# A trunk layer step with split weights: low parts written over the raw tile, six buffers of high parts, splits five tiles ahead, experts in pairs

## The chip, the cores and the metric

The kernel runs on one core of one Trainium2 chip. The metric is the device time in microseconds of one execution. Engines are named as in the profile: PE is TensorE (PEld its weight loads), DVE is VectorE, ACT is ScalarE, POOL is GpSimd, SP is SyncE, which here issues nearly all DMAs.

## The reference, cut to what matters

Two layers over 272 prompt rows (16 meta tokens and 256) and 32 rows of running sequences, model width 1024, feed-forward width 2816, all in fp32:

```python
for i in range(2):
    h = pool_mixer(x) if i == 0 else conv_module(x)            # layer 1: two dense products and a 31-tap conv
    x = layer_norm(ALPHA * x + h)
    f = swiglu(x) if i == 0 else moe_swiglu(x)                 # top 2 of 8 experts
    x = layer_norm(ALPHA * x + f)

def swiglu(x, wg, wu, wd):
    return (silu(x @ wg) * (x @ wu)) @ wd

def moe_swiglu(x, router, wg, wu, wd):
    gate = softmax over the two largest of x @ router, 0 elsewhere
    return sum(gate[:, e] * swiglu(x, wg[e], wu[e], wd[e]) for e in range(8))
```

## The kernel before, in words

A product in fp32 is made of three products in a faster format (fp32r): each operand is split into a high part (a cast) and a low part (the operand minus the high part), and high by high, high by low and low by high are summed in PSUM. For weights this goes tile by tile. A tile is 128 x 2048 floats, 1 MB. SP loads it into one of 11 raw buffers (`RAW`; the dense stages use 4 of them, `DENSE`), ACT casts it into `w_hi` (`hi`, line 546), DVE subtracts into `w_lo` (`lo`, line 1185), and PE uses both. There are three pairs of `w_hi` and `w_lo` (`SPLIT`). Tiles are numbered in the order of their use, and four semaphores count them: `raw_landed`, `hi_ready`, `split_ready`, `tile_used`. A cast of tile t waits until tile t - 3 is used; a load into a raw buffer waits until the tile that was in it is split (`split_ready`).

The dense stages come first: 22 gate and up tiles, 11 down tiles, 8 tiles of the first and 4 of the second product of the conv module (T_DOWN, T_W1, T_W2 are their first numbers). A dense tile is 48 matmuls of 304 columns. For the conv module's 31 taps, ACT also builds diagonal matrices, some of them in buffers of `w_hi` and `w_lo` (`diag`).

Then come 8 experts of 33 tiles each (`TE`), from T_MOE on. Each expert's rows are gathered by a product with a selection matrix (`gather_rows`, `gather_turn`), so that an expert works on 128 rows. For each of 11 column blocks j there are a gate tile and an up tile (24 matmuls of 256 columns each: the wide tiles), a transposition of h (`turn_h`), and the down tile of the block before (12 matmuls of 512 columns). The result yy of an expert is split into yy_hi (ACT, line 795) and yy_lo (DVE, line 1583), spread back to all rows behind the next expert's first up tile (`scatter`, line 1073), and added into `acc` by DVE bank by bank (`add_scattered`, line 1533). The gate tile of block 1 writes the bank that the scatter filled first, so PE waits there for the first add.

Every engine has its own instruction stream in a written order; nothing is reordered by a scheduler. ACT and DVE run casts and subtractions two or three tiles ahead of PE (`AHEAD`), interleaved by hand with evacuations. Seven experts run in a hardware loop (`Fori`), one per turn, and the eighth is written out after it. A second pass for experts with more than 128 rows follows under an `If`, which is skipped here.

Of the kernel before, what the change touches and what calls it, by code (L numbers as in the profile page):

```python
# [33 lines left out]
RAW = 11  # L34
SPLIT = 3
LN_EPS = 1e-5
# [4 lines left out]
def build_trunk(nc, x_prompt, x_sample, state_pool, state_conv, meta, pool_w, pool_scale, conv_w1,  # L41
# [34 lines left out]
    TE = 3 * NJ  # L76
    assert TE % RAW == 0 and TE % SPLIT == 0

# [18 lines left out]
    with ExitStack() as ctx:  # L97

        ring_at = 16512
        split_at = ring_at + RAW * 8192  # L100
        const_at = split_at + 2 * SPLIT * 8192
        place = [const_at]
# [255 lines left out]
        A_U = A_CONV + len(U_JOBS)  # L358
        AHEAD = 3
        SCAT = 6 * (E + 1)  # L360
# [13 lines left out]
        def diag(j):  # L374
            if j < EARLY:
                return diag_h[j], diag_l[j]
            if j < EARLY + SPLIT:
                k = (T_W2 + j - EARLY) % SPLIT
                return w_hi[k], w_lo[k]
            return diag_h[j - EARLY - SPLIT], diag_l[j - EARLY - SPLIT]  # L380

# [3 lines left out]
        def _(sp):  # L385
            def load(t, src, dst):

                if t >= DENSE:
                    sp.wait_ge(split_ready, load_ahead(t) + 1)
                sp.dma_start(dst(raw[raw_slot(t)]), src).then_inc(raw_landed[raw_slot(t)], 16)  # L390
# [51 lines left out]

            def load_expert(n, e, j):
                t = T_MOE + j
                sp.wait_ge(split_ready, n * TE + (t - RAW + 1))
                src, dst = expert_tile(e, j) if j < TE else expert_tile(e + 1, j - TE)
                sp.dma_start(dst(raw[raw_slot(t)]), src).then_inc(raw_landed[raw_slot(t)], 16)
# [20 lines left out]
            def one_pass(r):  # L468
                with sp.Fori(0, E - 1) as e:
                    for j in range(LENT, TE + LENT):  # L470
                        load_expert(r * E + e, e, j)
                for j in range(LENT, TE):
                    load_expert(r * E + (E - 1), E - 1, j)

# [57 lines left out]
        def _(act):  # L532
# [3 lines left out]
            def hi(t, n=None):  # L536

                landed = 16 * (loads_before(t) + 1)
                if n is None:
                    act.wait_ge(raw_landed[raw_slot(t)], landed)  # L540
                    if t >= SPLIT:
                        act.wait_ge(tile_used, t - SPLIT + 1)
# [142 lines left out]
            for i in range(NW1 // 2):  # L685
                if i < NW1 // 2 - 1:
                    hi(T_W1 + 2 * i + 2)
                    hi(T_W1 + 2 * i + 3)
                else:
                    uc_split(0)  # L690
                    uc_split(1)
                    act.wait_ge(tile_used, T_W2 - SPLIT + 1)
# [11 lines left out]
            act.wait_ge(tile_used, T_W2 - SPLIT + 2)  # L704
            diagonals(EARLY + 1, 0, 32)
            for k, (part, half) in enumerate(U_JOBS):
# [3 lines left out]
                         ps[U_BANKS[k]][0:n, :]).then_inc(evac_a, 1)  # L710
            act.wait_ge(tile_used, T_W2 - SPLIT + 3)
            diagonals(EARLY + 2, 0, 32)
# [44 lines left out]

            def one_expert(r, e, last):

                n = r * E + e  # L760
                t0 = n * TE

                def silu(j, gate_tile):
# [33 lines left out]
            def one_pass(r):  # L797
                rows_evac(r * E)
                xg_evac(r * E)
                with act.Fori(0, E - 1) as e:  # L800
                    one_expert(r, e, False)
                one_expert(r, E - 1, True)

# [3 lines left out]
            with act.If(largest > P):  # L807
                with act.Fori(1, 3) as r:
                    for j in range(AHEAD):
                        hi(T_MOE + j, r * E)  # L810
# [9 lines left out]
        def _(pe):  # L820
# [83 lines left out]
            def feature_block(banks, n, t, blocks, x_base=None):  # L904

                wh, wl = wide(w_hi[t % SPLIT]), wide(w_lo[t % SPLIT])
                for c in range(KC):
# [27 lines left out]
            for i in range(NJ):  # L937
                t = T_DOWN + i
                pe.wait_ge(split_ready, t + 1)
                pe.wait_ge(jlo_done, i + 1)  # L940
                wh, wl = tall(w_hi[t % SPLIT]), tall(w_lo[t % SPLIT])
                for s in range(TR):
# [133 lines left out]

            def one_expert(r, e, last):

                n = r * E + e
                scattered = r * SCAT + e * 6  # L1080

                def rows_block(bank, j, t):

                    pe.wait_ge(split_ready, n * TE + (t + 1))
                    wh, wl = wide(w_hi[t % SPLIT]), wide(w_lo[t % SPLIT])
                    for c in range(KC):
# [13 lines left out]
                def down(j, t):  # L1100
                    pe.wait_ge(split_ready, n * TE + (t + 1))
                    pe.wait_ge(ht_lo_done, n * NJ + (j + 1))
                    wh, wl = tall(w_hi[t % SPLIT]), tall(w_lo[t % SPLIT])
                    for s in range(TR):
# [8 lines left out]
                for j in range(NJ):  # L1113
                    g = T_MOE + (3 * j - 1 if j else 0)
                    if j == 0:
# [34 lines left out]
                if not last:  # L1150
                    gather_turn(n + 1)
                down(NJ - 1, T_MOE + TE - 1)

            def one_pass(r):
                gather_rows(r * E)
                gather_turn(r * E)
                with pe.Fori(0, E - 1) as e:
                    one_expert(r, e, False)
                one_expert(r, E - 1, True)
                scatter((r * E + E) * 2 + r + 1)  # L1160
# [12 lines left out]
        def _(dve):  # L1173
# [369 lines left out]

            def one_expert(r, e, last):

                n = r * E + e

# [9 lines left out]

                lo(T_MOE + 3, n)
                mult(0, 1)
                dve.wait_ge(h_done, n * NJ + (FC + 1))  # L1560
                add_scattered(e, r * SCAT + e * 6, range(4))
                for j in range(1, NJ):
                    g = 3 * j - 1
                    lo(T_MOE + g + 2, n)
# [3 lines left out]
                    lo(T_MOE + g + 3, n)  # L1568
                    mult(j, g + 1)
                    if not last or j < NJ - 1:  # L1570
                        lo(T_MOE + g + 4, n)
                    if j == 2 and not last:
# [3 lines left out]
                if not last:  # L1576
                    xg_low(n + 1)
                    lo(T_MOE + TE + 1, n)
                    lo(T_MOE + TE + 2, n)
                for k in range(2):  # L1580
# [5 lines left out]
            def one_pass(r):  # L1586
                with dve.Fori(0, E - 1) as e:
                    one_expert(r, e, False)
                one_expert(r, E - 1, True)
                dve.wait_ge(summed, r * SCAT + 6 * E)  # L1590
# [16 lines left out]
            with dve.If(largest > P):  # L1607
                with dve.Fori(1, 3) as r:
# [6 lines left out]
                    select(0)  # L1615
                    for j in range(AHEAD):
                        lo(T_MOE + j, r * E)
# [47 lines left out]
```

## Time and profile before

| | us |
|---|---|
| median of 3 runs | 1303.0 (1302.25 to 1303.61) |
| the profiled execution | 1302.67 |
| its span | 1300.9 |
| PE busy | 1243.0 (96%) |
| DVE busy | 1027.0 (79%) |
| ACT busy | 825.3 (63%) |

The span is what the profiler sees between the first and the last instruction; the execution has 1.8 us around it. The dense stages take up to about 440 us, the experts run from 456 to 1277 us, and a last normalization ends at 1301. The busy share of an engine is a mean over these stages; what each engine waits for is read stage by stage.

### The profile page before, as it was taken

The numbers are of one execution on the slowest core, as the hardware profiler recorded it, in microseconds if no ns is written. First come the engines' busy times: TensorE is split into PE (matmuls) and PEld (weight loads), VectorE is DVE, ScalarE is ACT, GpSimd is POOL, SyncE is SP. The second block draws the span as 40 slices with busy tenths as digits, with TensorE's granted clock in tenths as the row PEclk, the third lists the DMA queues.
The fourth block names the chain that finished last, engine by engine and source line by source line (L and its number), as shares of the span: only waits on it lengthen the run. The fifth ranks groups of instructions, "written<-read, shape, count | busy, mean of one in ns | idle before, by whom it ended". The sixth has DMA issues, their size and how long they took to land.

```text
span 1300.9 us, 22335 instructions
## 1 busy us (share of the span) xinstructions
PE 1243.0 (96%) x8651; PEld 1158.3 (89%) x8651; DVE 1027.0 (79%) x1064; ACT 825.3 (63%) x979; POOL 5.4 (0%) x22
## 2 busy tenths in 40 slices
PE   6999999999998899999999999999999999999992
PEld 4899999989988689989989989989998999998991
DVE  6687444467996688888888888889889879888886
ACT  3636563344876657767767767767776776776771
POOL 0000000000000000000000000000000000000000
PEclk9999999999999999999999999999999999999997
DMA  9355544422565169989989989999999998998931
GB/s 252 98 167 177 154 153 155 147 85 65 174 216 182 65 212 366 362 280 366 365 276 361 364 292 352 364 316 322 365 322 318 367 353 284 367 362 278 367 117 38
DMA packets 249537, 332.65 MB, mean 256 GB/s; under 512 B 6404, under 2 KB 222820, under 8 KB 249450
## 3 DMA queue, kind: packets, MB, share of 16 engines
q1 hardware_dynamic: 249283, 331.28, 75.8%
q10 hardware_dynamic: 199, 0.62, 0.2%
q8 instruction: 36, 0.59, 0.2%
q14 instruction: 19, 0.16, 0.0%
HBM read 330.44 MB, written 2.84 MB: 256 GB/s over the span
## 4 chain that ended last, share of the span: by engine, by line
PE 84%; DVE 10%; ACT 3%; issue 2%; DMA 0%; DVEq 0%; SPq 0%; ACTq 0%
PE bank L1088 36%; PE bank L1108 19%; PE bank L915 17%; PE bank L946 6%; DVE cacc L1368 2%; PE bank L1052 2%; PE bank L1097 1%; PE bank L1073 1%; ACT w_hi L546 1%; PE bank L854 1%; DVE acc L1533 1%; PE bank L900 1%; DVE sg L1265 1%; DVE yy_lo L1583 1%; DVE w_lo L1185 1%
## 5 line engine op out<-in xcount | busy, mean ns | idle before, releaser
L1185 DVE TENSOR_TENSOR w_lo<-raw,w_hi 128x2048 fp32r<-128x2048 f32 x309 | 707.8, 2291 | 184.3 <-ACT w_hi L546 183.6
L546 ACT CAST w_hi<-raw 128x2048 fp32r<-128x2048 f32 x309 | 591.1, 1914 | 226.1 <-PE bank L915 76.5
L1088 PE MATMUL bank<-w_hi,xg_hi 128*128 128x256 f32 x1408 | 400.7, 285 | 5.5 <-DVE acc L1533 3.7
L1088 PE MATMUL bank<-w_hi,xg_lo 128*128 128x256 f32 x1408 | 393.3, 279 | 0.0
L1088 PE MATMUL bank<-w_lo,xg_hi 128*128 128x256 f32 x1408 | 393.1, 279 | 0.0
L1088 PEld LDWEIGHTS bank<-w_hi,xg_hi 128*128 128x128 f32 x1408 | 264.5, 188 | 13.3 <-issue 9.1
L1088 PEld LDWEIGHTS bank<-w_lo,xg_hi 128*128 128x128 f32 x1408 | 265.0, 188 | 3.2
L1088 PEld LDWEIGHTS bank<-w_hi,xg_lo 128*128 128x128 f32 x1408 | 264.2, 188 | 0.0
L915 PE MATMUL bank<-x_hi,w_hi 128*128 128x304 f32 (+1 forms) x544 | 166.0, 305 | 6.9 <-DVE x_lo L1272 3.6
L915 PE MATMUL bank<-x_hi,w_lo 128*128 128x304 f32 (+1 forms) x544 | 164.0, 302 | 0.0
L915 PE MATMUL bank<-x_lo,w_hi 128*128 128x304 f32 (+1 forms) x544 | 163.2, 300 | 0.0
L1108 PE MATMUL bank<-w_hi,ht_hi 128*128 128x512 f32 x352 | 139.1, 395 | 1.3 <-DVE ht_lo L1555 1.0
L1108 PE MATMUL bank<-w_lo,ht_hi 128*128 128x512 f32 x352 | 138.2, 393 | 0.0
L1108 PE MATMUL bank<-w_hi,ht_lo 128*128 128x512 f32 x352 | 137.8, 392 | 0.0
L770 ACT CAST ht_hi<-bank 128x256 fp32r<-128x256 f32 x88 | 32.8, 373 | 135.3 <-PE bank L1097 135.3
L915 PEld LDWEIGHTS bank<-x_hi,w_hi 128*128 128x128 f32 x544 | 102.2, 188 | 9.0 <-issue 6.3
L915 PEld LDWEIGHTS bank<-x_lo,w_hi 128*128 128x128 f32 x544 | 102.5, 188 | 0.1
L915 PEld LDWEIGHTS bank<-x_hi,w_lo 128*128 128x128 f32 x544 | 102.3, 188 | 0.0
L1108 PEld LDWEIGHTS bank<-w_hi,ht_lo 128*128 128x128 f32 x352 | 66.2, 188 | 14.8
L1108 PEld LDWEIGHTS bank<-w_hi,ht_hi 128*128 128x128 f32 x352 | 66.1, 188 | 14.6 <-DVE ht_lo L1555 2.0
L1108 PEld LDWEIGHTS bank<-w_lo,ht_hi 128*128 128x128 f32 x352 | 66.2, 188 | 11.0
L946 PE MATMUL bank<-h_hi,w_hi 128*128 128x304 f32 x176 | 55.0, 313 | 1.9 <-DVE h_lo L1342 1.9
(202 smaller groups left out, 1279.5 us busy)
## 6 DMA issues: line engine op xcount, KB each, us to landing
raw<-in_moe_w_gate_dram SPq DMA_DIRECT2D x88, 1024.0 KB, 5.6
raw<-in_moe_w_up_dram SPq DMA_DIRECT2D x88, 1024.0 KB, 6.0
raw<-in_moe_w_down_dram SPq DMA_DIRECT2D x88, 1024.0 KB, 5.2
raw<-in_conv_w_dram SPq DMA_DIRECT2D x12, 1024.0 KB, 5.6
raw<-in_ffn_w_gate_dram SPq DMA_DIRECT2D x11, 1024.0 KB, 5.3
raw<-in_ffn_w_up_dram SPq DMA_DIRECT2D x11, 1024.0 KB, 5.4
raw<-in_ffn_w_down_dram SPq DMA_DIRECT2D x11, 1024.0 KB, 4.9
poolw<-in_pool_w_dram SPq DMA_DIRECT2D x1, 1024.0 KB, 10.8
```

Source lines behind the costliest of these rows:

```text
L546: act.copy(w_hi[t % SPLIT][:], raw[raw_slot(t)][:]).then_inc(hi_ready, 1)
L770: act.copy(ht_hi[:], ps[4 + j % 2][:, 0:TR * P].rearrange("p (c n) -> p c n", c=TR))\
L854: last = pe.matmul(ps[0][:, 0:n], mean_mat[:], z(c), start=(c == first), stop=(c == end))
L900: last = pe.matmul(ps[1][:, 0:n], mean_mat[:], sq[:, c, 0:n], start=(c == 0), stop=(c == KC - 1))
L915: last = pe.matmul(bank[:, 0:n], w[:, c, cols], x[:, c, 0:n], start=(c == 0 and k == 0), stop=(c == KC - 1 and k == 2))
L946: last = pe.matmul(ps[c][:, 0:NT], w[:, s, cols], x[i % 2][:, s, :], start=(i == 0 and s == 0 and k == 0), stop=(i == NJ - 1 and s == TR - ...
L1052: last = pe.matmul(ps[1 + 2 * half][:, :], sel[:, i, :], x[:, i, half * HALF:(half + 1) * HALF], start=(i == 0 and m == 0), stop=(i == 2 a ...
L1073: last = pe.matmul(ps[SCATTER_BANKS[k]][0:n, :], sel_t[:, P * i:P * i + n], y[:, half * HALF:(half + 1) * HALF], start=(m == 0), stop=(m = ...
L1088: last = pe.matmul(bank[:, 0:TW], x[:, c, :], w[:, c, :], start=(c == 0 and k == 0), stop=(c == KC - 1 and k == 2))
L1108: last = pe.matmul(ps[6 + half][:, :], x[:, s, :], w[:, s, cols], start=(j == 0 and s == 0 and k == 0), stop=(j == NJ - 1 and s == TR - 1 ...
L1185: dve.tensor_tensor(w_lo[t % SPLIT][:], raw[raw_slot(t)][:], w_hi[t % SPLIT][:], ALU.subtract).then_inc(split_ready, 1)
L1368: ins = dve.scalar_tensor_tensor(out=out, in0=src, scalar=v(V_DW + KC * k + q), in1=out, op0=ALU.mult, op1=ALU.add)
```

## The change

`w_lo` now lies at the addresses of `raw`, so the subtraction overwrites the raw tile, and the room that it had makes six buffers of `w_hi` (`HIGH`). A cast of tile t waits until tile t - 6 is used. A load into a raw buffer waits until the tile that was in it is used, not split. In the experts ACT and DVE run five tiles ahead (`AHEAD = 5`; three are split before the experts, as before, and two more on entering them). A buffer's number depends on the tile's number modulo 6 and an expert has 33 tiles, so the loops' bodies now hold two experts (`side` 0 and 1): three turns, and the last two experts are written out. The diagonal matrices of the conv module use six `w_hi` buffers in place of three pairs.

```diff
-SPLIT = 3
+HIGH = 6
-        w_hi = [at(f"w_hi{i}", [P, 2048], F32R, split_at + 16384 * i) for i in range(SPLIT)]
-        w_lo = [at(f"w_lo{i}", [P, 2048], F32R, split_at + 16384 * i + 8192) for i in range(SPLIT)]
+        w_lo = [at(f"w_lo{i}", [P, 2048], F32R, ring_at + 8192 * i) for i in range(RAW)]
+        w_hi = [at(f"w_hi{i}", [P, 2048], F32R, split_at + 8192 * i) for i in range(HIGH)]
-        AHEAD = 3
+        AHEAD = 5
+        EARLY_TILES = 3
 # SP
-                    sp.wait_ge(split_ready, load_ahead(t) + 1)
+                    sp.wait_ge(tile_used, load_ahead(t) + 1)
-                sp.wait_ge(split_ready, n * TE + (t - RAW + 1))
+                sp.wait_ge(tile_used, n * TE + (t - RAW + 1))
-                with sp.Fori(0, E - 1) as e:
-                    for j in range(LENT, TE + LENT):
-                        load_expert(r * E + e, e, j)
+                with sp.Fori(0, E // 2 - 1) as d:
+                    for j in range(LENT, 2 * TE + LENT):
+                        load_expert(r * E + 2 * d, 2 * d, j)
 # ACT, the cast
-                    act.wait_ge(tile_used, n * TE + (t - SPLIT + 1))
-                act.copy(w_hi[t % SPLIT][:], raw[raw_slot(t)][:]).then_inc(hi_ready, 1)
+                    act.wait_ge(tile_used, n * TE + (t - HIGH + 1))
+                act.copy(w_hi[t % HIGH][:], raw[raw_slot(t)][:]).then_inc(hi_ready, 1)
 # ACT, one expert (DVE alike, with lo)
+                def ahead(j):
+                    if not last or j < TE:
+                        hi(m0 + j, pair)
-                hi(T_MOE + 3, n)
+                ahead(AHEAD)
                 silu(0, 0)
                 for j in range(1, NJ):
                     g = 3 * j - 1
-                    hi(T_MOE + g + 2, n)
+                    ahead(g + AHEAD - 1)
                     turn_evac(j - 1)
...
-                    hi(T_MOE + g + 3, n)
+                    ahead(g + AHEAD)
                     silu(j, g)
-                    if not last or j < NJ - 1:
-                        hi(T_MOE + g + 4, n)
+                    ahead(g + AHEAD + 1)
...
-                    hi(T_MOE + TE + 1, n)
-                    hi(T_MOE + TE + 2, n)
+                ahead(TE + AHEAD - 2)
+                ahead(TE + AHEAD - 1)
 # PE (ACT and DVE alike)
-                with pe.Fori(0, E - 1) as e:
-                    one_expert(r, e, False)
-                one_expert(r, E - 1, True)
+                with pe.Fori(0, E // 2 - 1) as d:
+                    for side in range(2):
+                        one_expert(r, 2 * d, side, False)
+                for side in range(2):
+                    one_expert(r, E - 2, side, side == 1)
 # DVE, the subtraction
-                dve.tensor_tensor(w_lo[t % SPLIT][:], raw[raw_slot(t)][:], w_hi[t % SPLIT][:],
+                dve.tensor_tensor(w_lo[raw_slot(t)][:], raw[raw_slot(t)][:], w_hi[t % HIGH][:],
                                   ALU.subtract).then_inc(split_ready, 1)
```

The order on DVE (VectorE) where one expert ends and the next begins, before: two subtractions, the two halves of yy_lo, the loop's jump, one subtraction, then the product hn of block 0. The digits behind a name are the buffer and its place in the program.

```order
L1185 TENSOR_TENSOR w_lo1_64<-raw5_54,w_hi1_61 128x2048 [waits hi_ready]
L1184 REGISTER_ALU
L1185 TENSOR_TENSOR w_lo2_65<-raw6_55,w_hi2_62 128x2048 [waits hi_ready]
L1581 ISA
L1583 TENSOR_TENSOR yy_lo_140<-bank6,yy_hi_139 128x512 [waits yy_hi_done]
L1581 REGISTER_ALU
L1583 TENSOR_TENSOR yy_lo_140<-bank7,yy_hi_139 128x512 [waits yy_hi_done]
L1587 REGISTER_ALU
L1587 COMPARE_AND_BRANCH
L1185 TENSOR_TENSOR w_lo0_63<-raw7_56,w_hi0_60 128x2048 [waits hi_ready]
```

The same place in the changed kernel, between the two experts of a pair:

```order
L1201 TENSOR_TENSOR w_lo7_67<-raw7_56,w_hi3_74 128x2048 [waits hi_ready]
L1200 REGISTER_ALU
L1201 TENSOR_TENSOR w_lo8_68<-raw8_57,w_hi4_75 128x2048 [waits hi_ready]
L1603 ISA
L1605 TENSOR_TENSOR yy_lo_151<-bank6,yy_hi_150 128x512 [waits yy_hi_done]
L1603 REGISTER_ALU
L1605 TENSOR_TENSOR yy_lo_151<-bank7,yy_hi_150 128x512 [waits yy_hi_done]
L1200 REGISTER_ALU
L1201 TENSOR_TENSOR w_lo9_69<-raw9_58,w_hi5_76 128x2048 [waits hi_ready]
```

The order is the same; the tiles are two later ones, `w_lo7` has the place of `raw7`, and there is no jump inside a pair.

The order on ACT (ScalarE) at the same boundary, before: two casts, the two halves of yy_hi, the jump, one cast, silu of block 0.

```order
L545 REGISTER_ALU [waits raw_landed5]
L546 CAST w_hi1_61<-raw5_54 128x2048 [waits tile_used]
L545 REGISTER_ALU [waits raw_landed6]
L546 CAST w_hi2_62<-raw6_55 128x2048 [waits tile_used]
L795 CAST yy_hi_139<-bank6 128x512 [waits tile_used]
L795 CAST yy_hi_139<-bank7 128x512
L800 REGISTER_ALU
L800 COMPARE_AND_BRANCH
L546 CAST w_hi0_60<-raw7_56 128x2048 [waits tile_used,raw_landed7]
```

And in the changed kernel, between the two experts of a pair:

```order
L548 REGISTER_ALU [waits raw_landed7]
L549 CAST w_hi3_74<-raw7_56 128x2048 [waits tile_used]
L548 REGISTER_ALU [waits raw_landed8]
L549 CAST w_hi4_75<-raw8_57 128x2048 [waits tile_used]
L801 REGISTER_ALU
L803 CAST yy_hi_150<-bank6 128x512 [waits tile_used]
L803 CAST yy_hi_150<-bank7 128x512
L549 CAST w_hi5_76<-raw9_58 128x2048 [waits tile_used,raw_landed9]
```

Here too the order stands; the buffers `w_hi3` to `w_hi5` are new, and each cast's wait for `tile_used` names an earlier tile than before.

## Rows read from the trace of the kernel before

**Rows 1.** The page, busy time of each engine (share of the span) and instructions.
```profile
PE 1243.0 (96%) x8651; PEld 1158.3 (89%) x8651; DVE 1027.0 (79%) x1064; ACT 825.3 (63%) x979; POOL 5.4 (0%) x22
```

**Rows 2.** Windows of the dense stage and one expert: us, busy, clock, DMA share, GB/s.
```profile
100.00:260.00 160.00, 158.07 (x1124) 157.85 (x1124) 77.79 (x54) 80.23 (x136) 0.00 (x0) 0.99 0.48 154
...
864.00:967.00 103.00, 102.40 (x718) 94.66 (x719) 89.33 (x68) 72.75 (x64) 0.00 (x0) 1.00 0.99 336
```

**Rows 3.** Waits from 864 to 967: who waited for whom, us, times, longest.
```profile
ACT ht_hi L770 <- PE bank L1097: 16.8, 11, 4.9
...
ACT w_hi L546 <- PE bank L1108: 8.2, 10, 0.8
...
PE bank L1088 <- DVE acc L1533: 0.5, 1, 0.5
```

**Rows 4.** Timeline of ACT between two experts: start, us, instruction [idle before].
```profile
864.52 1.92 ACT L546 CAST w_hi<-raw 128x2048 fp32r<-128x2048 f32 x1
867.07 1.91 ACT L546 CAST w_hi<-raw 128x2048 fp32r<-128x2048 f32 x1 [0.64 <-PE bank L1108]
868.89 1.07 ACT L795 CAST yy_hi<-bank 128x512 fp32r<-128x512 f32 x2
```

**Rows 5.** Timeline of DVE at the same place.
```profile
866.46 2.29 DVE L1185 TENSOR_TENSOR w_lo<-raw,w_hi 128x2048 fp32r<-128x2048 f32 x1 [1.00 <-ACT w_hi L546]
869.02 2.29 DVE L1185 TENSOR_TENSOR w_lo<-raw,w_hi 128x2048 fp32r<-128x2048 f32 x1 [0.26 <-ACT w_hi L546]
...
872.43 2.28 DVE L1185 TENSOR_TENSOR w_lo<-raw,w_hi 128x2048 fp32r<-128x2048 f32 x1
874.63 0.41 DVE L1551 TENSOR_TENSOR hn<-sgn,bank 128x256 f32<-128x256 f32 x1
875.27 1.41 DVE L1533 SCALAR_TENSOR_TENSOR acc<-bank,gate,acc 128x512 f32<-128x512 f32 x2 [0.23 <-PE bank L1073]
```

**Rows 6.** Timeline of PE behind the scatter of that boundary.
```profile
875.20 0.40 PE L1073 MATMUL bank<-yy_lo,sel_t 128*32 128x512 f32 x1
876.15 0.39 PE L1088 MATMUL bank<-w_hi,xg_hi 128*128 128x256 f32 x1 [0.55 <-DVE acc L1533]
```

**Rows 7.** Timeline of DVE in the first expert.
```profile
456.02 0.91 DVE L1602 MEMSET yy_hi<- 128x1024 f32 x1 [0.16 <-issue]
...
463.91 1.41 DVE L1533 SCALAR_TENSOR_TENSOR acc<-bank,gate,acc 128x512 f32<-128x512 f32 x2 [0.24 <-DVE hn L1551]
```

**Rows 8.** Timeline of DVE in a normalization: one in place, one not.
```profile
286.90 0.53 DVE L1279 SCALAR_TENSOR_TENSOR zT<-zT,vec,sg 128x304 f32<-128x304 f32 x1
287.35 0.53 DVE L1272 SCALAR_TENSOR_TENSOR x_lo<-zT,vec,x_hi 128x304 fp32r<-128x304 f32 x1
```

**Rows 9.** All loads into raw buffers, time from issue to landing.
```profile
DMA to landing us min/median/max: 4.7/5.6/15.6
```

**Rows 10.** Timeline of PE: first and last matmuls of experts' first tiles.
```profile
866.64 0.39 PE L1108 MATMUL bank<-w_hi,ht_lo 128*128 128x512 f32 x1
866.87 0.28 PE L1088 MATMUL bank<-w_hi,xg_hi 128*128 128x256 f32 x1
...
869.58 0.28 PE L1088 MATMUL bank<-w_hi,xg_lo 128*128 128x256 f32 x1
...
969.76 0.28 PE L1088 MATMUL bank<-w_hi,xg_hi 128*128 128x256 f32 x1
...
972.36 0.28 PE L1088 MATMUL bank<-w_hi,xg_lo 128*128 128x256 f32 x1
...
1072.64 0.28 PE L1088 MATMUL bank<-w_hi,xg_hi 128*128 128x256 f32 x1
...
1175.52 0.28 PE L1088 MATMUL bank<-w_hi,xg_hi 128*128 128x256 f32 x1
```

**Rows 11.** Timeline of DVE behind the skipped second pass.
```profile
1290.21 0.34 DVE L1624 BATCH_NORM_AGGREGATE mv<-stats 128x2 f32<-128x12 f32 x3 [3.78 <-issue]
```

**Rows 12.** The page, one instruction queue: packets, MB, share.
```profile
q8 instruction: 36, 0.59, 0.2%
```

More of the change, by code:

```diff
@@ L76, in build_trunk @@
     TE = 3 * NJ
-    assert TE % RAW == 0 and TE % SPLIT == 0
+    assert 2 * TE % RAW == 0 and 2 * TE % HIGH == 0
     DENSE = 4
@@ L756, in rows_evac, with one_expert @@
                     act.copy(xg_rows[:, k * HALF:(k + 1) * HALF], ps[1 + 2 * k][:, :]).then_inc(rows_out, 1)
-            def one_expert(r, e, last):
-                n = r * E + e
+            def one_expert(r, first, side, last):
+                pair = r * E + first
+                n = pair + side
                 t0 = n * TE
+                m0 = T_MOE + side * TE
+                def ahead(j):
+                    if not last or j < TE:
+                        hi(m0 + j, pair)
                 def silu(j, gate_tile):
@@ L799, in one_pass @@
                 xg_evac(r * E)
-                with act.Fori(0, E - 1) as e:
-                    one_expert(r, e, False)
-                one_expert(r, E - 1, True)
+                for j in range(EARLY_TILES, AHEAD):
+                    hi(T_MOE + j, r * E)
+                with act.Fori(0, E // 2 - 1) as d:
+                    for side in range(2):
+                        one_expert(r, 2 * d, side, False)
+                for side in range(2):
+                    one_expert(r, E - 2, side, side == 1)
             one_pass(0)
@@ L808, in _ @@
                 with act.Fori(1, 3) as r:
-                    for j in range(AHEAD):
+                    for j in range(EARLY_TILES):
                         hi(T_MOE + j, r * E)
@@ L1075, in scatter, with one_expert @@
                     last.then_inc(spread, 1)
-            def one_expert(r, e, last):
-                n = r * E + e
-                scattered = r * SCAT + e * 6
+            def one_expert(r, first, side, last):
+                pair = r * E + first
+                n = pair + side
+                m0 = T_MOE + side * TE
+                scattered = r * SCAT + (first + side) * 6
                 def rows_block(bank, j, t):
-                    pe.wait_ge(split_ready, n * TE + (t + 1))
-                    wh, wl = wide(w_hi[t % SPLIT]), wide(w_lo[t % SPLIT])
+                    pe.wait_ge(split_ready, pair * TE + (t + 1))
+                    wh, wl = wide(w_hi[t % HIGH]), wide(w_lo[raw_slot(t)])
                     for c in range(KC):
@@ L1100, in down @@
                 def down(j, t):
[L1101 removed]
+                    pe.wait_ge(split_ready, pair * TE + (t + 1))
                     pe.wait_ge(ht_lo_done, n * NJ + (j + 1))
[L1103 removed]
+                    wh, wl = tall(w_hi[t % HIGH]), tall(w_lo[raw_slot(t)])
                     for s in range(TR):
@@ L1151, in one_expert @@
                     gather_turn(n + 1)
-                down(NJ - 1, T_MOE + TE - 1)
+                down(NJ - 1, m0 + TE - 1)
             def one_pass(r):
@@ L1156, in one_pass @@
                 gather_turn(r * E)
-                with pe.Fori(0, E - 1) as e:
-                    one_expert(r, e, False)
-                one_expert(r, E - 1, True)
+                with pe.Fori(0, E // 2 - 1) as d:
+                    for side in range(2):
+                        one_expert(r, 2 * d, side, False)
+                for side in range(2):
+                    one_expert(r, E - 2, side, side == 1)
                 scatter((r * E + E) * 2 + r + 1)
@@ L1542, in xg_low, with one_expert, ahead @@
                                       xg_hi[:, 4 * k:4 * k + 4, :], ALU.subtract).then_inc(xg_lo_done, 1)
-            def one_expert(r, e, last):
-                n = r * E + e
+            def one_expert(r, first, side, last):
+                pair = r * E + first
+                n = pair + side
+                e = first + side
+                m0 = T_MOE + side * TE
+                def ahead(j):
+                    if not last or j < TE:
+                        lo(m0 + j, pair)
                 def mult(j, up_tile):
@@ L1563, in one_expert @@
                     g = 3 * j - 1
-                    lo(T_MOE + g + 2, n)
+                    ahead(g + AHEAD - 1)
                     if j == 1:
@@ L1567, in one_expert @@
                     turn_low(j - 1)
-                    lo(T_MOE + g + 3, n)
+                    ahead(g + AHEAD)
                     mult(j, g + 1)
-                    if not last or j < NJ - 1:
-                        lo(T_MOE + g + 4, n)
+                    ahead(g + AHEAD + 1)
                     if j == 2 and not last:
@@ L1586, in one_pass @@
             def one_pass(r):
-                with dve.Fori(0, E - 1) as e:
-                    one_expert(r, e, False)
-                one_expert(r, E - 1, True)
+                for j in range(EARLY_TILES, AHEAD):
+                    lo(T_MOE + j, r * E)
+                with dve.Fori(0, E // 2 - 1) as d:
+                    for side in range(2):
+                        one_expert(r, 2 * d, side, False)
+                for side in range(2):
+                    one_expert(r, E - 2, side, side == 1)
                 dve.wait_ge(summed, r * SCAT + 6 * E)
@@ L1615, in _ @@
                     select(0)
-                    for j in range(AHEAD):
+                    for j in range(EARLY_TILES):
                         lo(T_MOE + j, r * E)
```

38 lines of the change are left out of this document (19 added, 19 removed).

## The prediction

> **What bounds the kernel now.** I read the page's head first, then the windows by stage, then the waits of one expert, then the three engines' timelines around the change from one expert to the next.
>
> The head says that TensorE is busy 96% of the span [rows 1]. The windows say where the other 4% are not: a stretch of 103 us in the expert loop, about one expert, has 102.3 us of matmuls, and 160 us of the dense stage have 158.1 [rows 2]. So both long stages run at TensorE's pace, and whatever makes a split or a load earlier can only give back the gaps. The waits of one expert show how small these are [rows 3]: ScalarE's casts wait 8.2 us behind TensorE's down tiles alone for a buffer of high parts, but that is an engine ahead of schedule. TensorE itself is in the list with 0.5 us behind a VectorE add, and nowhere behind `split_ready`. The change removes waits of ScalarE and VectorE which TensorE does not feel, except where a chain through those two engines ends at TensorE. That is at the start of each expert.
>
> **The boundary of two experts, step by step.** ScalarE casts two tiles ahead (864.52 and 867.07), then the two halves of yy_hi [rows 4]. VectorE subtracts for the same two tiles, makes yy_lo, subtracts one more tile, multiplies hn, and then adds bank 1 into acc [rows 5]. TensorE needs bank 1 for the second gate tile, and starts it at 876.15 after 0.55 us of marked idle, released by this add [rows 6]; from its last scatter matmul, one matmul pace (0.23) after 875.20, the gap is 0.7 us.
>
> In this chain one wait goes. The second cast sat 0.64 us until TensorE had used the last down tile, since with three buffers tile t needs tile t-3 used. With six it needs t-6, used two tiles earlier, so the cast starts right behind the first. VectorE gains less than 0.64: its first subtraction (866.46) still waits for the first cast, which waits for nothing that changes. Two subtractions in a row start 2.20 us apart (872.43 to 874.63), so the second can start at 868.66 and not 869.02: 0.36 us; the bracket in its row says 0.26. I take 0.35. All behind it on VectorE follows directly: yy_hi, right behind the cast, is made 0.6 earlier than 868.89, and so is the cast for the next subtraction, so neither stops VectorE. The add is 0.35 earlier, and TensorE's tile starts at 875.80. What is late next is the add still, behind the third subtraction: the scatter ends near 875.4, so 0.4 us of the gap stays. Seven boundaries: 7 x 0.35 = **2.45 us gained** (1.8 to 2.5).
>
> **The first expert loses.** Before, VectorE had one subtraction between clearing yy_hi (456.02) and the first add at 463.91 [rows 7]. Now it has three there, since tiles 3 and 4 are split on entry and tile 5 in the expert. The clearing ends at 456.93; no cast waits for TensorE any more; three subtractions at 2.20 end their turn at 463.55, and the add comes 0.64 later, as 874.63 to 875.27 [rows 5]: 464.2. That is **0.3 us lost** (0 to 0.5).
>
> **Edits that I cost at nothing.** Writing the low part over its raw values: a subtraction in place should take what it took. The nearest rows are two scalar_tensor_tensor of one size, one in place (zT over zT) and one not (x_lo), 0.53 us both [rows 8]. Bounds: 0, and 0.1 us on each of the four subtractions in the boundary chain, +3 us in all.
>
> A raw slot now comes free when TensorE has used the tile and not when VectorE has split it. In the expert loop a load thus starts about a tile and a half later, and its cast is wanted 11 - 6 = 5 tiles after that, some 15 us at a mean of 103/33 = 3.1 us a tile. A load lands 5.6 us after its issue in the median and 15.6 at worst, which was at the start of the program [rows 9]. A late one eats lead of the splits first, and there are five tiles of that. In the dense stage a load now waits until the tile four before it is used; a tile there is 48 matmuls of 160/1124 = 0.142 us, 6.8 us [rows 2], so three tiles are 20 us against 5.6 + 1.9 + 2.3 of load, cast and subtraction. SP stands behind the waiting load with nothing but later loads, which need the same event later. If that cover were gone, each late tile would stop TensorE for the excess; I see no stretch where it is.
>
> The orders of ScalarE and VectorE inside an expert shift by two tiles, but the evacuations keep their places: ScalarE comes to ht_hi with time to spare (16.8 us of waiting for TensorE per expert [rows 3]), and VectorE spends 89.4 us of 103 [rows 2]; ht_lo stays as late behind its split as before.
>
> **The paired loop.** A pair's body runs as long as two experts, so there are two jumps back in place of six. The jumps cost nothing that I can see: expert starts follow each other by 102.89, 102.88 and 102.88 us, and the last of these was left without a jump [rows 10]. So nothing is gained by removing four. A jump over a body twice as long has no row. From below it is 0. From above it is the one place where an engine sits with only a long skip and a register load before it, 3.78 us of "issue" on VectorE before L1624 [rows 11]. If TensorE's jump is read while its last down tile of 12 matmuls runs, that covers 12 x 0.23 = 2.76 us (the step from 866.64 to 866.87 [rows 10]), and the 0.4 to 0.6 us of gap before the second gate tile swallows some more. So at the upper row a jump costs 3.78 - 2.76 - 0.6 = 0.4 us, two jumps **0.8 us**, which I take; 0 to 7.6 is kept for the range.
>
> Here the Trainium skill speaks against the change (Runtime: NRT & Kernel Launch, section Instruction fetch mechanics): TensorE's instruction memory holds 2048 instructions, refilled in blocks of 256, and a taken branch to a target outside what is held stalls until it has been fetched. One expert is about 720 matmuls with a weight load each, 1440, and fits; a pair is 2880 and does not. The trace agrees for the kernel before: its one large instruction queue moved 36 packets, 0.59 MB, which at the page's 16 KiB a block is some 9,200 instructions, while TensorE ran 2 x 8651 [rows 1, 12], so the loop was not fetched again on each turn. The page gives no price for the stall; by the rule there are two of them.
>
> **Sum.** -2.45 + 0.3 + 0.8 = -1.35 us on the profiled execution's 1302.67 (span 1300.9 and 1.8 around it): 1301.3. The median of the three runs is 1303.0, 0.3 above; on that, **1301.6 us**. What this measurement can tell from no change is about 0.2%, 2.6 us: the forecast is no change that can be told, on the fast side.
>
> **Rivals.**
> 1. *TensorE's pace moves.* The wide tiles of 24 matmuls come in two paces at the same granted clock of 1.00 [rows 2]: 2.71 us from first to last matmul (866.87 to 869.58) or 2.60 (969.76 to 972.36) [rows 10]. I count 138 of 176 at the slower one. No view says what sets it; the same tile of the loop has either. The faster ones lie mostly in the first third of an expert, after a stop, which may mean that how casts, subtractions and loads fall against the matmuls plays a part, and the change moves all three. If the 134 slow tiles not hidden behind the boundary chain all turned fast: 134 x 0.11 = 14.7 us, with the boundary 1287; a third of them, 1297. Against it: the first tile of an expert is split well ahead in each of them, and has either pace. The other way, some 26 fast tiles turned slow cost 2.9 us, 1304.5.
> 2. *The jump over the pair stalls in full, and the time is slower.* If TensorE's queue does not run past the jump, or VectorE's and ScalarE's own longer bodies stall too, two jumps cost up to 3.78 each, 7.6 in all: 1303.0 - 2.15 + 7.6 = 1308.4. It decides from an uncovered 1.1 us per jump on. For it: the skip's 3.78 is a real row, and VectorE's chain at the boundary has no slack, so a stall there goes straight through. Against it: the jumps of before cost nothing, on any of the engines.
> 3. *The change does nothing at the boundary*, because the first cast, the yy chain or the scatter is what counts after all: 1303 to 1304, with the first expert's loss and jumps.
> 4. *Subtractions in the ring or late loads stop TensorE*: +3 to +6 us, 1304 to 1307.
>
> **How the numbers follow.** Forecast, 1299.5 to 1303.5: 0.50, of which a fifth is more than 2.6 us faster. Pace faster, 1288 to 1299.5: 0.22. Jump stall, 1302.5 to 1309: 0.17, most of it over 1305.6. Rival 3: 0.04. Rival 4 and a slower pace, 1303.5 to 1307: 0.07. So faster 0.33, same 0.47, slower 0.20. The range 1294 to 1308 leaves out the deep end of the faster pace (about 0.1) and the worst stall (under 0.1).
>
> **What would show it.** In the profile after: ScalarE's waits for TensorE before casts nearly gone in the expert loop, with TensorE's busy time per expert as before; the second cast at a boundary directly behind the first; the tile after the scatter 0.35 us nearer to it; experts 102.5 us apart; expert starts at odd and even places of the pair showing what a jump costs. The forecast is wrong if wide tiles change their pace in number, if TensorE waits for `split_ready`, or if every second boundary is longer by microseconds.

## The result and the profile after

| | before | after |
|---|---|---|
| median | 1303.6 us (7 runs, 1302.25 to 1307.45) | 1311.1 us (7 runs, 1308.10 to 1313.72) |
| the profiled execution, its span | 1302.67, 1300.9 | 1312.02, 1310.3 |

The ratio over all runs is 1.0048 with a 95% interval of 1.003 to 1.0065, which is some 6 us; between the medians it is 7.5. The changed kernel is slower, where 1301.6 and a chance of 0.20 for slower were forecast. Its median lies above the forecast's range (1294 to 1308) and above the 1308.4 of rival 2. Of the later runs, one of before (2501.7 us) and one of e7 (3174.6 us) fell into a slow state and are in no figure below.

The page of after, the lines that answer to [rows 1, 12], and the subtraction's group (busy, mean ns):

```profile
PE 1248.0 (95%) x8651; PEld 1164.1 (89%) x8651; DVE 1017.1 (78%) x1064; ACT 807.7 (62%) x979; POOL 5.4 (0%) x22
...
q8 instruction: 76, 1.25, 0.4%
...
L1201 DVE TENSOR_TENSOR w_lo<-raw,w_hi 128x2048 fp32r<-128x2048 f32 x309 | 700.3, 2287 | 174.1 <-ACT w_hi L549 173.7
```

The instruction queue moved 76 packets and not 36. The subtraction in place takes 2287 ns, as it took before (2291 in the same line of before's page). The busy time of TensorE grew by 5 us with the same number of instructions, so some ran slower; 4.4 us of the span are idle on top.

Most of the idle time lies where the loop turns; the busy time grew there and in the first expert. The waits of after from 864 to 967, the stretch of [rows 3], list something that before does not have: TensorE idle with nothing that releases it.

```profile
PEld bank L1102 <- issue: 3.8, 1, 3.8
DVE hn L1574 <- PE bank L1102: 3.4, 1, 3.4
PE bank L1102 <- issue: 3.4, 1, 3.4
```

TensorE's timeline of after at that place, the boundary of [rows 10] between the fourth and the fifth expert, where the loop jumps back (start, us, instruction, idle before):

```profile
873.23 0.40 PE L1122 MATMUL bank<-w_hi,ht_lo 128*128 128x512 f32 x1
877.01 0.46 PE L1102 MATMUL bank<-w_hi,xg_hi 128*128 128x256 f32 x1 [3.38 <-issue]
877.27 0.42 PE L1102 MATMUL bank<-w_lo,xg_hi 128*128 128x256 f32 x1
877.49 0.41 PE L1102 MATMUL bank<-w_hi,xg_lo 128*128 128x256 f32 x1
877.70 0.41 PE L1102 MATMUL bank<-w_hi,xg_hi 128*128 128x256 f32 x1
...
881.33 0.28 PE L1102 MATMUL bank<-w_hi,xg_lo 128*128 128x256 f32 x1
881.44 0.28 PE L1102 MATMUL bank<-w_hi,xg_hi 128*128 128x256 f32 x1
...
886.92 0.28 PE L1102 MATMUL bank<-w_hi,xg_hi 128*128 128x256 f32 x1
```

The down tile's last matmul and the next tile's first were 0.23 us apart; now it is 3.78. The tile behind the stall takes 4.43 us (877.01 to 881.44) instead of 2.83. In what follows, the boundary is the time from the last down matmul of one expert to the first matmul of the next one's second gate tile: 13.69 us here (873.23 to 886.92), before 9.51 (866.64 to 876.15 [rows 10, 6]). Windows of after say why (the stretch and its length, busy time and instructions of PE, PEld, DVE, ACT and POOL, granted clock, DMA share, GB/s): the dense stage, the stall, the tile behind it, the tile after that, and the start of the first expert.

```profile
100.00:260.00 160.00, 158.07 (x1124) 157.85 (x1123) 76.58 (x54) 81.03 (x134) 0.00 (x0) 0.99 0.47 152
...
873.90:877.00 3.10, 0.00 (x0) 0.00 (x0) 3.10 (x2) 2.18 (x4) 0.00 (x0) 1.00 0.68 229
877.00:881.40 4.40, 4.38 (x24) 4.39 (x25) 3.94 (x4) 1.60 (x1) 0.00 (x0) 0.61 0.27 108
881.40:884.20 2.80, 2.80 (x27) 2.80 (x27) 0.00 (x0) 2.18 (x2) 0.00 (x0) 1.00 0.36 81
...
450.00:461.00 11.00, 8.10 (x35) 6.50 (x34) 6.32 (x16) 7.41 (x9) 0.00 (x0) 0.69 0.00 1
```

TensorE stands still for 3.4 us, and then the granted clock is 0.61: most of the tile runs at the lower level, 1.2 GHz, where a matmul of 256 columns takes 0.21 us and not 0.11. Then it is back at 1.00. The last row shows a low clock where there is no jump, in the gather and the first tile of the first expert; before had 1.00 in it:

```profile
450.00:461.00 11.00, 8.10 (x61) 7.16 (x60) 4.06 (x15) 4.78 (x8) 0.00 (x0) 1.00 0.00 1
```

At a boundary inside a pair there is no stall, and what was forecast is there. After, ScalarE and VectorE between the third and the fourth expert, and TensorE behind the scatter, to be held against [rows 4, 5, 6]:

```profile
768.68 3.73 ACT L549 CAST w_hi<-raw 128x2048 fp32r<-128x2048 f32 x2
772.30 1.08 ACT L803 CAST yy_hi<-bank 128x512 fp32r<-128x512 f32 x2
```
```profile
770.63 4.49 DVE L1201 TENSOR_TENSOR w_lo<-raw,w_hi 128x2048 fp32r<-128x2048 f32 x2 [1.00 <-ACT w_hi L549]
...
776.25 2.28 DVE L1201 TENSOR_TENSOR w_lo<-raw,w_hi 128x2048 fp32r<-128x2048 f32 x1
778.45 0.41 DVE L1574 TENSOR_TENSOR hn<-sgn,bank 128x256 f32<-128x256 f32 x1
779.08 2.73 DVE L1549 SCALAR_TENSOR_TENSOR acc<-bank,gate,acc 128x512 f32<-128x512 f32 x4 [0.22 <-DVE hn L1574]
```
```profile
770.81 0.39 PE L1122 MATMUL bank<-w_hi,ht_lo 128*128 128x512 f32 x1
...
779.22 0.40 PE L1085 MATMUL bank<-yy_lo,sel_t 128*32 128x512 f32 x1
779.96 0.38 PE L1102 MATMUL bank<-w_hi,xg_hi 128*128 128x256 f32 x1 [0.34 <-DVE acc L1549]
```

The two casts are one block, the two subtractions too, and TensorE's idle time before the second gate tile went from 0.55 to 0.34. The boundary takes 9.15 us (770.81 to 779.96), before 9.50 or 9.51 at all boundaries in the loop and 9.24 at the one behind it: 0.36 less, where 0.35 was forecast. Its last part, from the first scatter matmul on, is 3.27 us (776.69 to 779.96), before 3.58 or 3.59; but that part is also longer when the two tiles ahead of it run at the faster of their paces and the scatter starts earlier, so the whole boundary is the better measure.

**Where 9.4 us of span went**, by comparing the starts of the tiles in the two profiles. The first expert, up to its second gate tile: +2.6, since its low clock costs 3.0 up to the scatter and TensorE, being late, then saves 0.4 of waiting. The two jumps: 3.50 of stall, 1.37 of slow tile, 0.22 more in the up tile behind it and 0.81 of waiting for the add that the stall swallows make +4.28 at the first, 3.55 + 1.59 - 0.14 - 0.82 = +4.18 at the second, 8.5 together. The five boundaries without a jump: -0.38, -0.36, -0.37, -0.62 and -0.41, which is -2.1; the fourth of these lies in the loop before and behind it after. What is left of the whole span is +0.4, of which 0.3 arose before the experts.

### The profile page after: what moved, and what is told of

Read it like the earlier page. It is cut to its first block, busy times and chain, and to the rows that moved or that the text cites. A ratio compares the mean times of both kernels' runs of the same rounds, so it can differ in the third digit from the quotient of the medians.

```text
span 1310.3 us, 22137 instructions
## 1 busy us (share of the span) xinstructions
PE 1248.0 (95%) x8651; PEld 1164.1 (89%) x8651; DVE 1017.1 (78%) x1064; ACT 807.7 (62%) x979; POOL 5.4 (0%) x22
## 4 chain that ended last, share of the span: by engine, by line
PE 85%; DVE 10%; ACT 3%; issue 2%; DMA 0%; DVEq 0%; ACTq 0%; SPq 0%
PE bank L1102 38%; PE bank L1122 18%; PE bank L927 17%; PE bank L958 6%; DVE cacc L1384 2%; PE bank L1064 2%; PE bank L1111 1%; DVE w_lo L1201 1%; PE bank L1085 1%; ACT w_hi L549 1%; PE bank L866 1%; PE bank L912 1%; DVE sg L1281 1%; DVE acc L1549 1%; DMA xin<-in_x_prompt_dram 0%
## 5 line engine op out<-in xcount | busy, mean ns | idle before, releaser
L1201 DVE TENSOR_TENSOR w_lo<-raw,w_hi 128x2048 fp32r<-128x2048 f32 x309 | 700.3, 2287 | 174.1 <-ACT w_hi L549 173.7
L549 ACT CAST w_hi<-raw 128x2048 fp32r<-128x2048 f32 x309 | 582.3, 1916 | 106.5 <-DMA raw<-in_ffn_w_up_dram 40.1
L927 PEld LDWEIGHTS bank<-x_lo,w_hi 128*128 128x128 f32 x544 | 102.4, 188 | 0.1
```

The costliest lines, as they stand in the source:

```text
L549: act.copy(w_hi[t % HIGH][:], raw[raw_slot(t)][:]).then_inc(hi_ready, 1)
L927: last = pe.matmul(bank[:, 0:n], w[:, c, cols], x[:, c, 0:n], start=(c == 0 and k == 0), stop=(c == KC - 1 and k == 2))
L1201: dve.tensor_tensor(w_lo[raw_slot(t)][:], raw[raw_slot(t)][:], w_hi[t % HIGH][:], ALU.subtract).then_inc(split_ready, 1)
```

## The experiments

Theory A: TensorE's program for a pair of experts no longer stays where one expert's did, so it is fetched again after each jump back, and TensorE waits for it; the deeper splits bring what was forecast. Theory B: the low parts in the ring, and raw slots that come free later, cost the time. Others are named with the run that tests them. In each table row below, "before" is the kernel before in the same set of runs: 1305.0 us in the first four (31 runs), 1305.4 in the last four (34 runs). e1 has 8 runs, e7 11, the others 12.

| | median us | ratio to before, 95% interval |
|---|---|---|
| e1, before with a loop over pairs | 1309.3 | 1.0034, 1.002 to 1.0049 |
| e2, after written out on all engines | 1302.3 | 0.9976, 0.9965 to 0.9987 |
| e3, six buffers and five ahead in a loop over one expert | 1305.5 | 1.0002, 0.9992 to 1.0011 |
| e4, before with low parts in place | 1304.8 | 0.9999, 0.9988 to 1.0011 |
| e5, after, TensorE alone written out | 1301.5 | 0.9972, 0.9955 to 0.9989 |
| e6, after, all but TensorE written out | 1309.7 | 1.0037, 1.0023 to 1.0051 |
| e7, before written out | 1303.3 | 0.9987, 0.9969 to 1.0004 |
| e8, as e3 but four ahead | 1302.6 | 0.9979, 0.9967 to 0.9992 |

**e1: the loop over pairs alone.** On each engine of the kernel before (cut; SyncE likewise with its loads):

```diff
-with pe.Fori(0, E - 1) as e:
-    one_expert(r, e, False)
+with pe.Fori(0, E // 2 - 1) as d:
+    for side in range(2):
+        one_expert(r, 2 * d + side, False)
+one_expert(r, E - 2, False)
 one_expert(r, E - 1, True)
```

> The kernel before with one edit: the loop's body holds two experts (two jumps back instead of six on each engine); three high and three low buffers, splits three tiles ahead, raw slots freed by the split. Theory A (the two jumps back over the pair stall TensorE, about 3.5 us idle and 1.5 us of half clock each, less 0.8 of the boundary's gap): 1303.6 + 2 x 4.2 = 1312 us, q8 instruction about 76 packets, and TensorE idle at the boundaries before the third and the fifth expert and at no other. Theory B (the low parts in the raw slots, and the slots freed later, cost the time): 1303.6. Theory C (the first expert's lower clock is brought by the deeper splits): the first expert at full clock here, whatever the total.

Measured: 1309.3, 4.3 us above before, and 76 packets in the queue. The place is right, the price was too high. The second jump in e1's timeline of TensorE, and the windows of this stall and of the tile behind it:

```profile
872.34 0.40 PE L1113 MATMUL bank<-w_hi,ht_lo 128*128 128x512 f32 x1
875.25 0.38 PE L1093 MATMUL bank<-w_hi,xg_hi 128*128 128x256 f32 x1 [2.52 <-DVE w_lo L1192]
...
884.05 0.38 PE L1093 MATMUL bank<-w_hi,xg_hi 128*128 128x256 f32 x1
```
```profile
872.30:875.20 2.90, 0.44 (x2) 0.00 (x1) 2.65 (x2) 2.42 (x3) 0.00 (x0) 1.00 0.24 81
875.20:878.10 2.90, 2.85 (x24) 2.85 (x25) 2.90 (x3) 0.45 (x1) 0.00 (x0) 1.00 0.84 243
```

The stall is 2.5 us here and not 3.4 (the releaser in its bracket is inferred; the tile that TensorE starts was split long before). The clock stays at 1.00. This boundary takes 11.71 us (872.34 to 884.05) and the one of the first jump 11.81, against 9.51: 2.3 and 2.2 us for the jumps, 4.5 in all, and a boundary that now lies behind the loop gives 0.26 back. That is 4.2, and the medians are 4.3 apart. So the loop alone makes the kernel slower, without any other part of the change. Theory B's 1303.6 is out. Theory C falls too: e1 has no deeper splits, and the first expert's low clock is in its profile (0.71 from 450 to 461).

**e2: no loop.** In all four engines of after, in the first pass (in outline, SyncE likewise with its loads):

```diff
-with pe.Fori(0, E // 2 - 1) as d:
-    for side in range(2):
-        one_expert(r, 2 * d, side, False)
+for d in range(E // 2 - 1):
+    for side in range(2):
+        one_expert(r, 2 * d, side, False)
```

> The kernel after without its loop: the eight experts of the first pass are written out on all four engines, buffers and lookahead as after. Theory A: no jump back, so no stall at the boundaries, 1311.1 - 8.4 = 1302.7 us if the first expert's half clock (2.9 us) stays, 1300 if it was chance; 0.35 us gained at each of the seven boundaries. Theory B (the in-place low parts cost the time): 1311. Theory D (code that is read for the first time stalls TensorE as a jump does): 1311 or more, with idle time before every expert.

Measured: 1302.3, with 71 packets, nearly as many as after. TensorE's first boundary in e2:

```profile
556.89 0.39 PE L1136 MATMUL bank<-w_hi,ht_lo 128*128 128x512 f32 x1
557.11 0.28 PE L1116 MATMUL bank<-w_hi,xg_hi 128*128 128x256 f32 x1
...
565.71 0.38 PE L1116 MATMUL bank<-w_hi,xg_hi 128*128 128x256 f32 x1
```

No stall stands at any boundary, so the packets alone cost nothing that can be seen where the code runs straight on; only the jump waits. Theory D falls. All boundaries take 8.82 us, 0.69 less than in the loop before, which is nearly twice the forecast 0.35; e7 says where the rest is from.

**e3: the loop over one expert with six buffers.** 33 tiles do not divide by six, so the order of the buffers is a table (cut; a cast waits for the tile that last had its buffer, and the other engines loop alike):

```diff
+HIGH_OF = [j % 6 if j < 18 else (j - 18) % 5 for j in range(TE)]
-act.copy(w_hi[t % HIGH][:], raw[raw_slot(t)][:])
+act.copy(w_hi[high(t)][:], raw[raw_slot(t)][:])
-with act.Fori(0, E // 2 - 1) as d:
+with act.Fori(0, E - 1) as e:
```

> The kernel after with a loop over one expert as in the kernel before: the six high buffers are taken in the order 0 to 5 three times, then 0 to 4 three times, so that 33 tiles close the cycle and a buffer comes back after at least five tiles. In-place low parts and splits five tiles ahead stay. Theory A: the body fits again, so q8 instruction is near 36 packets, no stall, 1303.6 - 7 x 0.35 = 1301 us (1304 if the first expert's half clock is brought by the deeper splits). Theory B: 1309 to 1311.

Measured: 1305.5, the same as before, 36 packets, no stall, and no gain: the boundaries take 9.51 us as before. The miss has its reason in ScalarE's timeline of e3 at the first boundary:

```profile
558.94 1.92 ACT L558 CAST w_hi<-raw 128x2048 fp32r<-128x2048 f32 x1
561.50 1.92 ACT L558 CAST w_hi<-raw 128x2048 fp32r<-128x2048 f32 x1 [0.64 <-PE bank L1129]
```

At the end of an expert the table gives a buffer back after five tiles, and five ahead of the last down tile means waiting for that tile: the wait of [rows 4] to the hundredth. Depth alone is worth nothing here; what counts, as e8 shows, is that no cast at the boundary waits for the last down tile. (Its profile has the first expert's low clock as well, 0.69.)

**e4: low parts in place alone.** In the kernel before (cut; the dense stages' loads wait for `tile_used` too, and the diagonal matrices get buffers in the room of `w_lo`):

```diff
-w_lo = [at(f"w_lo{i}", [P, 2048], F32R, split_at + 16384 * i + 8192) for i in range(SPLIT)]
+w_lo = [at(f"w_lo{i}", [P, 2048], F32R, ring_at + 8192 * i) for i in range(RAW)]
-sp.wait_ge(split_ready, n * TE + (t - RAW + 1))
+sp.wait_ge(tile_used, n * TE + (t - RAW + 1))
```

> The kernel before with one edit: the low part is written over the raw values and a load waits until TensorE has used the tile; three high buffers, splits three tiles ahead, a loop over one expert stay. Theory A: 1303.6, the same within 0.2%; subtraction 2.29 us as before. Theory B (in-place writing or the later freeing costs the time): 1309 to 1311.

Measured: 1304.8 against 1305.0, the same. This is theory B's own test, and it falls.

**e5 and e6: whose jump.** The edit of e2 on TensorE alone (e5), and on the other three engines alone (e6).

> The kernel after, with the first pass written out for TensorE alone; ScalarE, VectorE and SyncE keep the loop over pairs. Theory A (it is TensorE's own jump that stalls): no idle 3.4 us before the third and the fifth expert, 1311.1 - 2 x 4.2 = 1302.7 us. Theory E (the jump of another engine holds TensorE up at the same place): at least one of the two stalls stays, 1306 to 1311.

> The kernel after, with the first pass written out for ScalarE, VectorE and SyncE; TensorE alone keeps the loop over pairs. Theory A: both stalls stay, 1302.3 (all written out) + 2 x 4.2 = 1310.7 us. Theory E: they go, 1302 to 1306.

Measured: 1301.5 and 1309.7, theory A's numbers to within 1.2 us. TensorE's timelines at the boundary of the second and the third expert in e5, and of the fourth and the fifth in e6:

```profile
659.95 0.39 PE L1122 MATMUL bank<-w_hi,ht_lo 128*128 128x512 f32 x1
660.18 0.28 PE L1102 MATMUL bank<-w_hi,xg_hi 128*128 128x256 f32 x1
```
```profile
870.39 0.39 PE L1136 MATMUL bank<-w_hi,ht_lo 128*128 128x512 f32 x1
874.11 0.50 PE L1116 MATMUL bank<-w_hi,xg_hi 128*128 128x256 f32 x1 [3.33 <-issue]
```

With TensorE written out nothing stands at the boundary, though the three others jump there; with TensorE alone in a loop the stall is whole. The windows of e6 show the tile behind each of its two stalls at a low clock again:

```profile
664.80:669.10 4.30, 4.29 (x24) 4.29 (x25) 3.97 (x4) 0.62 (x1) 0.00 (x0) 0.64 0.22 88
...
874.10:878.60 4.50, 4.49 (x25) 4.49 (x26) 4.00 (x4) 0.65 (x1) 0.00 (x0) 0.62 0.23 93
```

**e7: before, written out.** The edit of e2 in the kernel before.

> The kernel before with the first pass written out on all four engines; its three high and three low buffers and splits three tiles ahead stay. Theory F (part of what the written-out kernel gained at a boundary comes from the loop itself: the boundary that before has behind its loop took 3.22 us against 3.58 in it): six boundaries at 3.22, 1305.0 - 6 x 0.36 = 1302.8 us. Theory G (all of it comes from the deeper splits): 1305.0.

Measured: 1303.3, a ratio whose interval just reaches 1, with all boundaries at 9.29 or 9.30 us in its profile:

```profile
559.57 0.39 PE L1119 MATMUL bank<-w_hi,ht_lo 128*128 128x512 f32 x1
...
565.64 0.47 PE L1084 MATMUL bank<-yy_hi,sel_t 128*128 128x512 f32 x1 [0.24 <-DVE yy_lo L1598]
...
568.86 0.38 PE L1099 MATMUL bank<-w_hi,xg_hi 128*128 128x256 f32 x1 [0.21 <-DVE acc L1548]
```

So theory F holds in kind: writing out is worth 0.21 us a boundary by itself (9.51 to 9.30). From the first scatter matmul on it is the 3.22 us expected, 0.36 less than before, but the scatter itself starts later, after a wait for yy_lo, and 0.15 of the gain goes there. Six boundaries make 1.3 us and not 2.2; the total, 2.0 less than before, is not told from no change. The freed cast is worth 0.36 in the loop (after) and 0.48 written out (9.30 here to e2's 8.82), so each helps the other a little, and together they are e2's 0.69. In the loop the semaphore values are worked out in registers, written out they are constants; whether that is the 0.21, or something else about the loop, was not tried.

**e8: four ahead.** One number of e3:

```diff
-        AHEAD = 5
+        AHEAD = 4
```

> The one-expert loop with six high buffers, in place, but splits four tiles ahead instead of five: with buffers that come back after five tiles the last cast at a boundary then waits for the tile before the last down tile, not for that tile itself (in the run with five ahead this cast waited 0.64 us for the last down tile as in the kernel before, and the boundary took 3.58 us as before). Theory A: boundaries 3.58 to 3.27 in the loop and 3.22 to 2.95 behind it, 1305.0 - 6 x 0.31 - 0.27 = 1302.9 us. Theory H (the loop over one expert, not the cast's wait, keeps the boundary at 3.58): 1305.

Measured: 1302.6, a ratio of 0.9979, theory A. ScalarE's timeline at the first boundary, and TensorE's at the first and the sixth:

```profile
558.25 1.91 ACT L558 CAST w_hi<-raw 128x2048 fp32r<-128x2048 f32 x1
560.05 1.07 ACT L812 CAST yy_hi<-bank 128x512 fp32r<-128x512 f32 x2
```
```profile
558.57 0.39 PE L1129 MATMUL bank<-w_hi,ht_lo 128*128 128x512 f32 x1
...
566.99 0.40 PE L1092 MATMUL bank<-yy_lo,sel_t 128*32 128x512 f32 x1
567.72 0.38 PE L1109 MATMUL bank<-w_hi,xg_hi 128*128 128x256 f32 x1 [0.34 <-DVE acc L1554]
...
1070.88 0.39 PE L1129 MATMUL bank<-w_hi,ht_lo 128*128 128x512 f32 x1
...
1080.03 0.38 PE L1109 MATMUL bank<-w_hi,xg_hi 128*128 128x256 f32 x1 [0.54 <-DVE acc L1554]
```

No cast waits before yy_hi, TensorE's idle time at the first boundary is 0.34 as in the changed kernel, and that boundary takes 9.15 us (558.57 to 567.72). So do all six in the loop (9.15 or 9.16), and the one behind it takes 8.89: 0.35 less than before at each of the seven, which is the forecast's 2.45 us. At the sixth the idle time is 0.54, as before, since its first two tiles ran 0.2 us faster and TensorE came to the wait earlier; the boundary is the same (1070.88 to 1080.03). Theory H falls. This is the change's idea in a loop that fits, 2.8 us faster than before between the medians (1.0 to 4.3 by the interval). e2 and e5 are faster than both kernels too; e5 has the lowest median, and the three were not compared with each other closely enough to rank them.

## Why the prediction was wrong

**The step that failed** is the jump. The prediction said: "If TensorE's jump is read while its last down tile of 12 matmuls runs, that covers 12 x 0.23 = 2.76 us", and took 0.4 us a jump. There is no such cover: the idle time begins when the down tile ends (873.23 to 877.01 in after), and it is 3.4 us, bare, not far below the upper row's 3.78 [rows 11]. On top came what no term had: the tile behind the stall at a lower clock, 1.4 and 1.6 us. A jump cost 4.28 and 4.18 us, where the sum had 0.4 for each; two of them are 7.7 us more than the sum had. e5 shows that this is TensorE's jump and no other's, and e1 that it needs no other part of the change.

The reason against rival 2, "the jumps of before cost nothing", was read from jumps whose target was still held: 36 packets with six jumps back, 76 with two, and in before the queue moves no packet from 560 to 1180 us, over five jumps back. By the Trainium skill (Runtime: NRT & Kernel Launch, section Instruction fetch mechanics) a taken branch whose target is not in the current two-page window stalls until the target's page has been fetched; the traces of after, e1 and e6 agree, at 2.5 to 3.4 us a time. In before, e3 and e8 the body, one expert with about 718 matmuls and as many weight loads [rows 2], is longer than two of that section's blocks of 256 instructions, and the jump is free: there the traces differ, and for TensorE more than two blocks are held. The prediction had this rule, counted that a pair does not fit, and then priced it by a cover that it had not seen.

**The boundary's gain** was right in kind and size where it could show. The second cast stands right behind the first, yy_lo and the add come earlier, and the boundaries inside a pair in the loop are 0.36 to 0.38 shorter against 0.35 forecast; e8 shows the gain alone, with experts 102.4 to 102.5 us apart where 102.5 was forecast. Two of the seven boundaries are those of the jumps, where the stall swallows the whole gap, 0.8 us each, and the gain with it; the sum had counted it there.

**The first expert** was forecast to lose 0.3. In after it can't be seen, since TensorE comes late itself. In e2, e5 and e6, which have the same three subtractions there and the clock at 1.00, the first add comes 8.34, 8.53 and 8.35 us after the clearing of yy_hi begins, against 7.89 before: 0.5 to 0.6 late, where 0.3 was forecast.

**Edits at nothing**: the subtraction in place (2287 ns) and the raw slots freed later (e4, the same time) cost nothing, and TensorE waits for a split only where it did before, once, at 405 us, for 1.1 us in both. Rival 1 (TensorE's pace) came in number but not in time: 151 of the 176 wide tiles are at the slower pace (by the median step between their matmuls), before 138. Six of the 13 are in the first expert, where the tiles behind the second gate tile make +0.3 us; elsewhere the pace changed only in the first two tiles of an expert, where as a rule a wait follows that hides it. Rival 2 was right, under-sized at 3.78 a jump since it had no slow tile. Rivals 3 and 4 did not come.

**The first expert's low clock** is in the profiles of after, e1 and e3 (0.69 to 0.71 from 450 to 461) and in none of before, e2, e4, e5, e6, e7 and e8 (1.00). No part of the change separates the two groups: e5 and e6 have after's buffers and depth without it, e1 has the buffers of before with it. It makes 2.6 us of the 9.4 between the two profiles, and runs of one kernel spread by 3 to 9 us. Without it the profiles differ by 6.8 us, the medians by 7.5 here and by 6.1 against the 31 later runs of before. What brings it in one run and not in another stays open.

## What to carry to other kernels

Before a loop's body is made longer, count TensorE's instructions in it, and look at the instruction queue's packets: if the body no longer fits, each turn costs a bare stall (2.5 to 3.4 us here, and more where the clock falls behind it), and a jump that is free in the short loop says nothing about it. A buffer that is to free a chain from a wait is judged by the one wait in that chain, not by depth: with a buffer back after five tiles, five ahead gained nothing and four ahead gained 0.35 us a boundary. To see such a gain, measure a stretch whose start the change does not move: from the scatter on, half of e8's boundaries in the loop seem to have gained only 0.1 us. Where the loop is the obstacle, write out the engine that stalls (e5), or find an order of buffers that closes within the short loop (e8).

## What the runs showed of the hardware

- From the packet of the instruction queue to TensorE's first matmul behind the jump it is about the same time in two kernels. At the first jump the packet lies between 664.25 and 664.50 in after and between 664.50 and 664.75 in e1, and TensorE starts at 667.48 and 667.51, 3 us later in both. The idle time differs (3.33 and 2.60) because the packet comes at a different point of the down tile: 0.5 to 0.75 us after its last matmul began in after, with it in e1. What sets that point is open.
- After idle times of 3.33 to 3.38 us (two in after, two in e6) the next tile took 4.09 to 4.47 us, at a granted clock of 0.61 to 0.64 in the three windows shown. After those of 2.52 and 2.60 us (e1) it took 2.92 and 2.93, at 1.00 in the one shown. So a stall that was 0.8 us longer had 1.2 to 1.5 us more behind it; no run changes the length of the stall alone.
- Code that runs straight on is fetched without a stall at the boundaries: 71 packets in e2, e5 and e7, against 76 in after.
